# Two attention branches of a transformer block merged into one mixed stage of 16 units

## The reference, cut to what matters

```python
u = rmsnorm(x, norm_mix) * (1 + scale1) + shift1
aq, ak, av, bq, bkv, biq, bik, biw, cq, ck, cv, g = split_cols(u @ w_in)
y_a = diff_attention(aq, ak, av, lam, lam_init, diff_subln, bias_a) @ w_br_a
y_b = dsa_attention(bq, rmsnorm(bkv, dsa_kv_norm), biq, bik, biw, dsa_w_uv, bias_b) @ w_br_b
y_c = moba_attention(cq, ck, cv, bias_c) @ w_br_c
merged = gates_0 * y_a + gates_1 * y_b + gates_2 * y_c
x = x + gate1 * (merged @ w_o)
```

## Time and profile before

| | us |
|---|---|
| median of 3 runs | 1864.11 |
| lowest, highest | 1857.58, 1868.36 |
| the profiled execution, its own time | 1860.6 |
| its span in the trace | 1858.7 |

### The profile page before, as it was taken

How to read it: one execution, slowest core, us unless ns; L and a number is a source line. 1 busy time by engine, 2 the same in 40 slices (tenths; PEclk the granted TensorE clock), 3 DMA queues, 4 the chain that set the end, 5 groups by cost and what they waited for, 6 DMA issues and landing times.

```text
span 1858.7 us, 22342 instructions
## 1 busy us (share of the span) xinstructions
PE 1715.8 (92%) x8605; PEld 1414.5 (76%) x8605; DVE 1038.0 (56%) x1326; ACT 791.7 (43%) x963; POOL 96.7 (5%) x143
## 2 busy tenths in 40 slices
PE   6999978899999999989898989999899887789996
PEld 6788867688888788889855777888688673668885
DVE  4577654466655676645554435555548653655553
ACT  4434433365434444333455335555444433334441
POOL 1000000010000000010000003000100010200000
PEclk8999989999999999999899999999899895799998
DMA  8687734177864677633400425556365330536550
GB/s 288 201 277 262 233 108 157 40 255 252 268 226 147 229 259 262 225 104 101 167 33 1 139 69 174 190 189 213 108 231 204 109 106 1 170 125 203 181 181 23
DMA packets 210195, 311.74 MB, mean 168 GB/s; under 512 B 16537, under 2 KB 145589, under 8 KB 209872
## 3 DMA queue, kind: packets, MB, share of 16 engines
q1 hardware_dynamic: 204112, 288.90, 46.6%
q0 software_dynamic: 6016, 21.94, 3.4%
HBM read 306.59 MB, written 4.21 MB: 167 GB/s over the span
## 4 chain that ended last, share of the span: by engine, by line
PE 85%; DVE 6%; ACT 3%; issue 3%; DMA 1%; PEld 1%; POOL 1%; DVEq 0%; PEldq 0%; ACTq 0%; SPq 0%; POOLq 0%
PE ps L1994 24%; PE ps L1996 24%; PE ps L1995 24%; DVE wlo L1304 1%; PE ps L2035 1%; PE ps L2330 1%; PE ps L2116 1%; PE ps L2217 1%; PE ps L2315 1%; DMA area<-in_gate_b 1%; PE ps L2045 1%; PE ps L2198 1%; PE ps L2418 1%; PE ps L2306 1%; ACT xn L811 0%
## 5 line engine op out<-in xcount | busy, mean ns | idle before, releaser
L1304 DVE TENSOR_TENSOR wlo<-raw,whi 128x2048 fp32r<-128x2048 f32 x255 | 581.0, 2298 | 238.1 <-ACT whi L757 237.3
L757 ACT ACTIVATE whi<-raw 128x2048 fp32r<-128x2048 f32 x255 | 481.2, 1910 | 207.1 <-PE ps L1996 183.7
L1994 PE MATMUL ps<-wlo,aT_hi 128*128 128x512 f32 (+1 forms) x1280 | 500.2, 391 | 22.1 <-DVE aT_lo L1330 9.2
L1996 PE MATMUL ps<-whi,aT_hi 128*128 128x512 f32 (+1 forms) x1280 | 493.4, 385 | 0.0
L1995 PE MATMUL ps<-whi,aT_lo 128*128 128x512 f32 (+1 forms) x1280 | 493.0, 385 | 0.0
L1994 PEld LDWEIGHTS ps<-wlo,aT_hi 128*128 128x128 f32 x1280 | 244.1, 191 | 72.6 <-issue 15.0
L1996 PEld LDWEIGHTS ps<-whi,aT_hi 128*128 128x128 f32 x1280 | 243.5, 190 | 47.9
L1995 PEld LDWEIGHTS ps<-whi,aT_lo 128*128 128x128 f32 x1280 | 244.2, 191 | 45.1
L1994 PE MATMUL ps<-wlo,hT_hi 128*128 128x512 f32 x480 | 188.0, 392 | 5.4 <-DVE hT_lo L1421 3.0
L1996 PE MATMUL ps<-whi,hT_hi 128*128 128x512 f32 x480 | 187.6, 391 | 0.0
L1995 PE MATMUL ps<-whi,hT_lo 128*128 128x512 f32 x480 | 187.3, 390 | 0.0
(11 more groups left out here) (302 smaller groups left out, 1388.4 us busy)
## 6 DMA issues: line engine op xcount, KB each, us to landing
raw<-in_ffn_w_in SPq DMA_DIRECT2D x176, 512.0 KB, 4.9
raw<-in_ffn_w_out SPq DMA_DIRECT2D x88, 512.0 KB, 4.3
raw<-in_w_ff SPq DMA_DIRECT2D x64, 512.0 KB, 4.7
raw<-in_ada_w SPq DMA_DIRECT2D x48, 512.0 KB, 5.5
raw<-in_w_in SPq DMA_DIRECT2D x48, 512.0 KB, 4.7
raw<-in_xattn_w_kv SPq DMA_DIRECT2D x32, 512.0 KB, 7.0
raw<-in_xattn_w_q SPq DMA_DIRECT2D x16, 512.0 KB, 4.8
raw<-in_xattn_w_o SPq DMA_DIRECT2D x16, 512.0 KB, 4.9
```

The source lines that it names most:

```text
L757: act.activation(to, of, ACT.Copy).then_inc(hi_ready[slot], 1)
L1304: dve.tensor_tensor(lo, of, hi, ALU.subtract).then_inc(lo_ready[slot], 1)
L1994: pe.matmul(o, lh, rl, start=start, stop=False, skip_group_check=True)
L1996: return pe.matmul(o, lh, rh, start=False, stop=stop, skip_group_check=True)
```

## The change

It touches the stages from `wide_inputs` to `merge` only.

1. Bias 0 is turned inside `wide_inputs` after its ninth chunk, bias 1 and bias 2 inside `sparse_inputs` (after its first and second chunk), into banks 6 and 7; bias 2 goes to a buffer of its own. The stages `diff_bias`, bias 1, bias 2 are gone.
2. `diff`: 4 matmuls of a zero tile (`keep_clock`, 128x512) ahead of each unit's score; a one-column Exp at ACT's entry.
3. The latent's norm, transposes and `kvT` copy run inside `sparse_inputs`.
4. POOL adds the selection mask to bias 1 once for each query tile (one add of 512 columns, one of 1024), where DVE added it in each of the 8 index units.
5. `dsa(0)`, `dsa(1)` and the 8 units of `moba` become one stage `sparse` with 16 units in a fixed mixed order, three ahead, four score banks, 3 zero matmuls ahead of each score from unit 4 on.
6. ACT and DVE make the high and low halves of each result inside `sparse`; PE goes into `merge` without an `enter()`. POOL's load of a norm gain (`load_gain(12)`) moves from before `wide_inputs` to `merge`.

```diff
@@ program
             e.wide_inputs()
-            e.diff_bias()
             e.diff()
             e.sparse_inputs()
-            e.latent()
-            e.dsa(0)
-            e.dsa(1)
-            e.moba()
+            e.sparse()
             e.merge()
@@ POOL, sparse_inputs
+                    pool.wait_ge(bias_turned, 2)
                     load_skew(2)
+                    pool.wait_ge(bias_kept, 4)
+                    pool.tensor_tensor(dsa_bias[0], bias[:, :, P:S], sel[0].to_broadcast([P, 4, P]), ALU.add).then_inc(masked, 1)
                     pool.wait_ge(summed, 3)
                     power(ss8[:, 0:2], rstd8[:, 0:2], 2, P).then_inc(powered, 1)
...
+                    pool.tensor_tensor(whole, whole, sel[1].unsqueeze(1).to_broadcast([P, 4, 2, P]), ALU.add).then_inc(masked, 1)
@@ ACT, diff
+                    act.activation(small[:, 62:63], minus_half[:, 0:1], ACT.Exp)
                     exps(0)
@@ ACT, sparse
+                    act.activation(aTf_hi[:, 0:1024], yTf[:, 0:1024], ACT.Copy).then_inc(aT_hi_made, 1)
+                    for u in range(3):
+                        exps(u)
+                    for u in range(16):
                         keep(u)
+                        if u + 3 < 16:
+                            exps(u + 3)
+                        if last_dsa(u - 1):
+                            keep_lat()
+                        if last_dsa(u - 2):
+                            out_hi()
@@ DVE, sparse
+                    for u in range(3):
+                        top(u)
+                    dve.wait_ge(aT_hi_made, c_turned.next())
+                    dve.tensor_tensor(aTf_lo[:, 0:1024], yTf[:, 0:1024], aTf_hi[:, 0:1024], ALU.subtract).then_inc(aT_made, 1)
+                    for u in range(16):
+                        weigh(u)
+                        if u + 3 < 16:
+                            top(u + 3)
@@ PE, wide_inputs
+                        if c == 8:
+                            pe.wait_ge(index_read, 2)
+                            self.turn_bias(0)
@@ PE, diff, score
+                        keep_clock(4, 2 * (u % 3))
@@ PE, sparse_inputs
                     chunk(0, 512, turned(bank()))
+                    self.turn_bias(1)
...
+                    pe.wait_ge(bias_kept, 4)
+                    self.turn_bias(2)
                     chunk(0, 512, turned(bank()))
-                    self.turn_bias(1)
@@ PE, sparse
+                    def score(u):
+                        kind, h, t, w = sparse_unit(u)
+                        if u >= 4:
+                            pe.wait_ge(maxed, units.n + u - 3)
+                            keep_clock(3, u % 4)
...
+                    for u in range(3):
+                        score(u)
+                    for u in range(16):
+                        if u + 3 < 16:
+                            score(u + 3)
+                        turn(u)
                         if u:
                             values(u - 1)
+                        if last_dsa(u - 2):
+                            expand()
@@ PE, merge
-                    enter()
+                    stages.next()
+                    pe.wait_ge(maxed, units.n)
```

More of the change, by code:

```diff
@@ L447, in skip @@
                     stages.next()
-                head = diff_bias = diff = latent = dsa = skip
-                def moba(self):
-                    stages.next(2)
+                head = diff = sparse = skip
                 def wide_inputs(self):
@@ L1104, in keep_bias @@
                     act.wait_ge(bias_turned, b + 1)
[L1105 to L1110, removed]
+                    to = moba_bias if b == 2 else bias
+                    act.activation(to[:, 0:2, :], ps[:, 6, :].rearrange("p (h k) -> p h k", h=2), ACT.Copy).then_inc(bias_kept, 1)
                 def exps(self, u, segs, U, depth=2):
@@ L1163, in keep_result, with sparse @@
                             act.wait_ge(branch_done, 1)
                             act.activation(yT[:, 0:2, :], ps[:, 2, :], ACT.Copy)
+                            self.keep_bias(2)
                     chunks(3, evac, after=keep_result)
                     leave()
+                def sparse(self):
                     enter()
[L1169 to L1176, removed]
@@ L1192, in dsa @@
[L1192 to L1213, removed]
-                        act.activation(moba_PT[u % 2][:, 0:w], ps[:, 5 + u % 2, 0:w], ACT.Copy).then_inc(probs_kept, 1)
-                    exps(0)
-                    exps(1)
-                    for u in range(8):
-                        keep(u)
-                        if u + 2 < 8:
-                            exps(u + 2)
-                    units.next(8)
@@ new lines, in score, with turn @@
+                        pe.matmul(ps[:, u % 4, 0:w], q, k, start=True, stop=True).then_inc(scored, 1)
+                    def turn(u):
+                        w = sparse_unit(u)[3]
+                        pe.wait_ge(weighed, units.n + u + 1)
+                        if u >= 2:
+                            pe.wait_ge(probs_kept, units.n + u - 1)
+                        for m in range(w // P):
+                            last = pe.transpose(ps[:, 4 + u % 2, P * m:P * m + P], Ps[u % 4][:, P * m:P * m + P], ident)
+                        last.then_inc(probs_turned, 1)
@@ L2524, in values @@
-                        last.then_inc(pv_done, 1)
-                    score(0)
-                    score(1)
-                    for u in range(8):
-                        if u + 2 < 8:
-                            score(u + 2)
-                        self.turn_probs(u, u % 2, 5 + u % 2, depth=3)
+                        if kind == "moba":
+                            j = mobas.next() - 1
+                            c = S * (h // 2) + P * t
+                            for m in range(t + 1):
+                                last = pe.matmul(ps[64 * (h % 2):64 * (h % 2) + 64, 6, c:c + P], cv[:, m, 64 * h:64 * h + 64],
+                                                 moba_PT[j % 2][:, P * m:P * m + P], start=m == 0, stop=m == t)
+                            last.then_inc(pv_done, 1)
+                            return
```

265 lines of the change are left out of this document (125 added, 140 removed).

## The result

The changed kernel took 1833.8 us, the median of 4 runs (1831.17 to 1838.54), against 1863.88 for the kernel before in the same series: a ratio of 0.9844, 95% interval 0.9806 to 0.9882. The profiled execution took 1831.17 us, span 1829.4.

A forecast was written before the change was run, and what follows sets the result against it. PE, busy for 92%, was taken as the bound, with time won where it stands still or its clock is low. Terms summed to -31.3 us from 1860.6, so 1829.3, with the median's 3.5 1833 us; own range 1826 to 1840.

The forecast's parts named there:

- B: diff: table load hidden and PE's work at full clock, 19.3 us against 22.42, so -3.1 us.
- B2: Projections behind diff: they start at full clock instead of holding 2 us at half, -1.0 us.
- C: Projections: biases 1 and 2 stand in PE's stream, +3.9 us; work added to other engines costs 0.
- E: Mixed stage of the sparse attentions: 51.9 us becomes 30.9, with one clock spell at its start, -21.0 us.
- A: Bias 0, ahead of diff: handover of 3.97 us becomes 2.85 with the bias matmuls in wide_inputs, -1.1 us.
- the term for PE's own work: diff: PE's 17.12 us busy, nearly all at half clock, halves to 8.6 at full clock.
- the tail: End of diff: about 1.9 us in which the last unit's chain has nothing over it.
- D: Handover from projections to the attentions: 8.36 us becomes about 1.35, -7.0 us.
- F: merge: 4 us at half clock in its 24.59 go, since it comes out of a busy PE, -2.0 us.
- 1, waits set the pace: Mixed stage: semaphore waits hold units at 2.19 us each, stage 38.6 us, +7.7, total 1840; chance 0.17.
- 2, the clock stays low: Mixed stage only: clock stays low, 52.2 us instead of 30.9, and merge's 2 us lost, total 1856; chance 0.08.
- 3, zeros as dead weight: diff and mixed stage: clock stays at 1.2 GHz, zeros lie on the path, diff 35.6 us, total 1873; chance 0.05.

The follow-up runs named there:

- e8: e7 with diff's zeros also moved into PE's waits (28 in all, where there were 32): 1821.73 us, 0.9794 of the kernel before.
- e1: The changed kernel without the four zero matmuls of each diff unit: 1832.6 us, 0.9848 of the kernel before.
- e10: The changed kernel with the block attention's bias turned at the start of the mixed stage, not in the projections: 1830.64 us, 0.9839 of the kernel before.
- e7: The changed kernel with the mixed stage's zeros taken out and ten put behind its third score: 1825.73 us, 0.9814 of the kernel before.
- e2: The changed kernel without the three zero matmuls of each mixed-stage unit: 1828.05 us, 0.9827 of the kernel before.
- e3: The changed kernel without the new zero matmuls in both diff and the mixed stage: 1828.06 us, 0.9823 of the kernel before.
- e9: e5 with the mixed stage's units broken into three pipelines (0 to 3, 4 to 7, 8 to 15): 1840.82 us, 0.9888 of the kernel before.
- e6: The changed kernel with the mixed stage's scores, maxima and exponentials two units ahead instead of three: 1833.43 us, 0.9863 of the kernel before.
- e4: The kernel before with only zeros added in diff and both sparse attentions, and the early table load: 1872.3 us, 1.0048 of the kernel before.
- e5: The changed kernel with the mixed stage's units reordered to eight dsa, then eight moba: 1829.55 us, 0.9836 of the kernel before.

## Why the prediction was right, and where it was not

The total (1833 forecast, 1833.8 measured) holds a miss of 3.0 us in B, one of 1.6 in B2 and C and one of 0.9 in E; in the profiled execution about 3 us of chance ahead of `diff` make up for much of it. So that the total came within 1 us is in part luck.

- **A, bias 0, -1.1.** `diff` starts 4.2 us earlier than before (1462.35 against 1466.54), but in the twelve traces of kernels with the same code up to there it starts between 1459.95 and 1466.32, with clock spells in other places. The term is neither contradicted nor confirmed; some 3 us of the profiled difference were chance.
- **B, `diff`, -3.1: wrong**, measured -0.1. The step that failed is "the load now runs while PE does zeros and the first score, and four zeros (0.9) stand ahead of that score: 4.2 us". It counted the first four zeros, not the second four, for which DVE's in-order queue makes `weigh(0)` wait: 5.21 us, so 1.0 of the miss. The other 2.0 lie behind the first transpose, in the term for PE's own work, "at full clock I halve it, 8.6". There PE was busy for 14.43 us instead of 12.2, with 2.7 of waits (2.9 forecast). The work does not halve: e8, at full clock, has 17.14 us busy with 28 zeros of 0.227 in it, which leaves 10.8. In the rows a transpose of 128x128 shows 0.47 us at half clock and 0.33 at full clock (the timeline above). Without zeros (e1) the stage took 21.10, with them in the waits (e8) 18.27.
- **B2, projections start at full clock, -1.0: wrong.** It took the clock to hold through the tail, the 1.9 us with nothing over them; that is just where it falls. 6.8 us at half clock followed, 4.2 of them in the projections. e8, with zeros in the tail, has the full clock.
- **C, projections, +3.9: right.** At full clock they take 35.93 (e8). Before, the projections had 33.26 at 0.97, or 32.3 with B2's 1.0 off: +3.7. POOL's adds (1.29 and 2.39 us, forecast 1.2 and 2.4) are hidden. They did not take twice their price; it was DVE that was slowed beside them (last section).
- **D, handover, -7.0: right**, 8.36 to 1.24. e10 shows that for the block attention's bias it is not the place that counts.
- **E, mixed stage, -21.0: right in size**, 51.9 to 31.77 (forecast 30.9), with one spell at half clock at its start. The first transpose came 3.24 us in (forecast 3.55), and PE was busy for 29.25. But the terms are not all right. PE's own work, taken as 18.5 at full clock, was at its upper bound: e7, at 1.00, has 22.06 us busy with ten zeros of 0.227 in it, which leaves 19.8. And the forecast read the zeros as what keeps the clock and so pays. e2 and e7 show that 8.2 us of zeros bought less than they cost.

  The tables of before and after part the 20.1 us. PE's idle time in these stretches fell from 15.6 us to 2.5, so 13.1. Its busy time fell from 36.3 to 29.25, so 7.0; as 2.0 of bias turn left the stretch and 8.2 of zeros came in, the same work took some 13 us less, at 0.95 in place of 0.50 to 0.57. The idle time is what one fill and drain in place of three, two stage handovers less and more units ahead removed; 2.99 + 3.81 = 6.8 us were bias 2's stage and the handover to merge, with 4.4 of that 15.6 in them. And the clock mostly followed from the order of work: without zeros the mixed stage had 0.71 and 0.76 (e3, e2). e9 puts back two fills and drains and loses 7.8 us, 3.4 of them idle. What three ahead gives over the one of `dsa` was not tried; over two it is some 1 us (e6). POOL's masks and the early halves of the results were not tried by themselves either.
- **F, merge, -2.0: right**, 24.59 to 22.84 at 1.00.
- **The rivals.** 1, waits set the pace: no; PE is busy for 92% of the stage. 2, the clock stays low: no. 3, zeros as dead weight: not here, but it is what e4 did in its profiled execution, where the clock fell in the handover ahead of the attentions and never came back in them. The argument against this rival, that dense zeros release the throttle, did not hold there.

## What to carry to other kernels

A pipeline's fills and drains, and the handovers beside them, cost more than its steady part shows: joining three short pipelines gave far more (7.8 us by e9, over half of it through the clock) than the order inside them (nothing that shows, e5). Filler matmuls belong behind the last instruction that another engine waits for and ahead of PE's own wait; ahead of a score they delay every in-order queue behind it, and at half clock they are dead weight. Judge them by taking them out: `diff` had a clock of 0.94 instead of 0.56 with its zeros and was longer. And look at more executions than one: a spell at half clock comes and goes between executions of one kernel.

## What the runs showed of the hardware that was not expected

- A busy PE does not always get its clock back. In e4 block attention ran for 25.86 us at 0.50 with PE busy for 24.86, with 15 zero matmuls of 128x512 among its work and scores on 64 of 128 rows. The clock came back some 6 us after merge's first 128x512 matmul, with PE busy throughout (a stretch of e4, with 1.00):

```profile
1603.60:1605.60 2.00, 2.00 (x10) 1.64 (x9) 0.07 (x1) 0.00 (x0) 1.58 (x1) 1.00 0.96 327
```

  The Trainium skill ("TensorE: Matmul & The Clock Gate", Part 1) says that activity releases the throttle. By busy time alone e4's block attention doesn't agree with it, while merge does; what made the difference was not tried by itself.
- Beside POOL's two-input add, DVE's two-input instructions are slower. In the kernel after, two scalings of 128x128 took 1.79 us beside an add on POOL; the same two took 0.61 in the kernel before, where POOL was idle. A copy, with one input, that ran just ahead of them beside the same add took 0.69, as it did elsewhere. The timelines of after and of before:

```profile
1510.57 2.39 POOL L704 TENSOR_TENSOR area<-area 128x1024 f32<-128x1024 f32 x1
1510.97 0.69 DVE L1770 COPY gain<-ps 128x512 f32<-128x512 f32 x1 [0.82 <-PE ps L2385]
1511.58 1.79 DVE L1838 SCALAR_TENSOR_TENSOR area<-area,small,xn 128x128 f32<-128x128 f32 x2
```

```profile
1528.53 0.61 DVE L1845 SCALAR_TENSOR_TENSOR area<-area,small,xn 128x128 f32<-128x128 f32 x2 [2.56 <-POOL small L541]
```
